# One-core decoder layer: mixer pieces in a new order, the first piece multiplied unsplit, weight halves split ahead of each evacuation, every head transposed during the next

## The reference

```python
def rmsnorm(t, g):
    t32 = t.astype(jnp.float32)
    t32 = t32 * lax.rsqrt(jnp.mean(t32 * t32, axis=-1, keepdims=True) + EPS)
    return (t32 * g.astype(jnp.float32)).astype(t.dtype)
...
    for _ in range(DEPTH):
        xn = rmsnorm(h, g_mix)
        proj = xn @ w_in
        q, k, v, u_pool, q_mem, gate_logits = jnp.split(proj, SPLITS, axis=-1)

        q = rotary(rmsnorm(q.reshape(B, S, DA_HEADS, 2, DA_HEAD_DIM), q_norm), cos, sin)
        k = rotary(rmsnorm(k.reshape(B, S, DA_HEADS, 2, DA_HEAD_DIM), k_norm), cos, sin)
        v = v.reshape(B, S, DA_HEADS, DA_V_DIM)
        o = diff_attention(q, k, v, lam)
        o = rmsnorm(o, g_subln) * (1.0 - LAMBDA_INIT)
        y_attn = o.reshape(B, S, V_DIM) @ w_b_attn

        y_pool = multiscale_pool(u_pool, pool_w, pool_scale) @ w_b_pool

        y_mem = memory_cross_attention(q_mem, mem, g_mem, w_mem_kv, mq_norm, mk_norm) @ w_b_mem

        g = jax.nn.sigmoid((gate_logits + b_gates).astype(jnp.float32)).reshape(B, S, N_BRANCHES, D)
        merged = (g[:, :, 0] * y_attn.astype(jnp.float32)
                  + g[:, :, 1] * y_pool.astype(jnp.float32)
                  + g[:, :, 2] * y_mem.astype(jnp.float32)).astype(h.dtype)
        h = h + merged @ w_out

        h = h + moe(rmsnorm(h, g_ffn), w_router, b_router, w_gate, b_gate,
                    w_up, b_up, w_down, b_down)
```

## Time and profile before

| | us |
|---|---|
| median of 3 runs | 1284.41 |
| lowest, highest | 1283.96, 1288.04 |
| the profiled execution, its own time | 1283.99 |
| its span, first to last instruction | 1280.7 |
| PE busy | 1174.9 (92%) |
| DVE busy | 464.4 (36%) |
| ACT busy | 251.4 (20%) |
| DMA, mean over the span | 358 GB/s |

### The profile page before, as it was taken

One profiled execution on the slowest core, in us unless ns is written; L12 is line 12 of the kernel. 1 busy time (PEld: TensorE's weight loads), 2 busy tenths in 40 slices (PEclk: granted clock), 3 DMA queues, 4 the chain that ended last, 5 costly groups with the idle time before them and its releaser, 6 DMA issues.

```text
span 1280.7 us, 13937 instructions
## 1 busy us (share of the span) xinstructions
PE 1174.9 (92%) x5444; PEld 589.1 (46%) x5444; DVE 464.4 (36%) x814; ACT 251.4 (20%) x378; POOL 20.8 (2%) x29
## 2 busy tenths in 40 slices
PE   6998999997899999999999999999999999999997
PEld 5786787775643343434334343434434333333332
DVE  7669778874531212122122222212221212212131
ACT  5443555542111010001001010100100010001100
POOL 0200000010000000000000000000000000000000
PEclk9998999998899999999999999999999999999999
DMA  8454454386679999999999999999999999999996
GB/s 317 173 172 149 137 199 165 132 295 230 278 293 420 387 404 428 427 431 427 427 431 427 427 431 427 427 431 427 427 431 427 427 431 427 427 431 427 427 431 285
DMA packets 54824, 458.50 MB, mean 358 GB/s; under 512 B 4304, under 2 KB 5200, under 8 KB 30224
## 3 DMA queue, kind: packets, MB, share of 16 engines
q1 hardware_dynamic: 53408, 454.15, 85.9%
q0 software_dynamic: 1104, 3.93, 0.9%
q10 hardware_dynamic: 288, 0.10, 0.0%
HBM read 457.11 MB, written 1.05 MB: 358 GB/s over the span
## 4 chain that ended last, share of the span: by engine, by line
PE 68%; DMA 16%; DVE 10%; ACT 3%; issue 2%; SPq 0%; DVEq 0%; ACTq 0%
PE bank L1496 29%; DMA experts_ring<-in_w_down 14%; PE bank L1548 14%; PE bank L1254 12%; PE bank L1516 5%; PE bank L1484 3%; DVE ring_split L776 3%; PE bank L1502 2%; ACT region L746 1%; PE bank L1223 1%; PE bank L1503 1%; DMA ring<-in_w_in 1%; DVE region L1174 1%; ACT prob L651 1%; ACT region L749 1%
## 5 line engine op out<-in xcount | busy, mean ns | idle before, releaser
L1496 PE MATMUL bank<-experts_ring,region 128*64 128x512 f32 x2048 | 454.0, 595 | 11.5 <-DVE region L1183 6.6
L1496 PEld LDWEIGHTS bank<-experts_ring,region 128*64 128x64 f32 x2048 | 145.0, 137 | 291.7 <-issue 286.8
L1548 PE MATMUL bank<-experts_ring,region 128*64 128x512 f32 x1024 | 228.8, 596 | 31.8 <-ACT region L746 25.0
L1254 PE MATMUL bank<-ring_split,region_split 128*128 128x512 f32 x768 | 233.7, 406 | 18.0 <-DVE ring_split L776 11.0
L1254 PEld LDWEIGHTS bank<-ring_split,region_split 128*128 128x128 f32 x768 | 146.8, 195 | 52.7 <-DVE ring_split L776 12.7
L1548 PEld LDWEIGHTS bank<-experts_ring,region 128*64 128x64 f32 x1024 | 73.1, 137 | 167.0 <-issue 125.8
L1254 PE MATMUL bank<-ring_split 128*128 128x512 f32 x288 | 114.7, 398 | 0.0
L1208 DVE COPY region<-bank 64x512 f32<-64x512 f32 x32 | 22.2, 694 | 237.0 <-PE bank L1548 237.0
L1191 DVE TENSOR_SCALAR region<-bank 128x512 f32<-128x512 f32 x32 | 22.1, 692 | 209.7 <-PE bank L1503 209.7
L776 DVE TENSOR_TENSOR ring_split<-ring,ring_split 128x2048 fp32r<-128x2048 f32 x42 | 95.7, 2288 | 0.3
L1198 DVE TENSOR_SCALAR region<-bank 128x512 f32<-128x512 f32 x32 | 22.1, 692 | 179.7 <-PE bank L1503 179.7
(11 more groups left out here) (167 smaller groups left out, 615.9 us busy)
## 6 DMA issues: line engine op xcount, KB each, us to landing
experts_ring<-in_w_gate SPq DMA_DIRECT2D x64, 2048.0 KB, 25.9
experts_ring<-in_w_up SPq DMA_DIRECT2D x64, 2048.0 KB, 25.1
experts_ring<-in_w_down SPq DMA_DIRECT2D x64, 2048.0 KB, 27.9
ring<-in_w_in SPq DMA_DIRECT2D x28, 1024.0 KB, 5.2
ring<-in_w_mem_kv SPq DMA_DIRECT2D x4, 1024.0 KB, 12.4
ring<-in_w_b_attn SPq DMA_DIRECT2D x4, 1024.0 KB, 5.1
ring<-in_w_out SPq DMA_DIRECT2D x4, 1024.0 KB, 5.0
region<-in_b_gates POOLq DMA_DIRECT2D x6, 512.0 KB, 5.2
```

Of the source, the lines that this page charges most:

```text
L1254: ins = nc.tensor.matmul(UB[u % 3][:, :], a[:, k, toks], b[:, cols], start=(k == 0 and m == 0), stop=(k == k_n - 1 and m == 2))
L1496: ins = nc.tensor.matmul(dst[h * SLOTS:(h + 1) * SLOTS, :], XE[:, kk, e * SLOTS:(e + 1) * SLOTS], w[:, k, h * HALF:(h + 1) * HALF], start= ...
L1548: ins = nc.tensor.matmul(bank[2][h * SLOTS:(h + 1) * SLOTS, :], AHT[:, k, half * SLOTS:(half + 1) * SLOTS], w[:, k, h * HALF:(h + 1) * HAL ...
```

## The change

The pieces are taken in another order. `SPLIT_AT` puts both parts of a half's split (`hi_after`, `lo_after`) ahead of a unit's evacuation, where they stood behind it. The first piece isn't split: its 16 matmuls take x and the weights in plain float32, and x itself is split by ACT (upper) and DVE (lower) later. Sums of squares come from ACT (`square_evac`), the inverse roots of all groups from POOL (`inverse_root`: an addition and a power), in place of ACT's root and DVE's reciprocal. For q the factor isn't multiplied in but given to the exponential as its scale. A head's outcome is squared by ACT, rooted by POOL, scaled out by ACT (`o_squares`, `o_out`), and transposed by PE in the following head's pass (`turn_o`). In the mixer's end, ACT's splits of the last halves go behind its copies of the merged sum, and unit 44 is cut in two with the last transposition between.

```diff
-PIECES = ["pool", "mk", "mv", "qm", "q0", "q1", "k0", "k1", "v0", "v1", "gp0", "gp1", "wbp",
+PIECES = ["pool", "mk", "q0", "mv", "q1", "qm", "k0", "v0", "k1", "v1", "gp0", "gp1", "wbp",
...
-UPPER_AT, LOWER_AT = {}, {}
+SPLIT_AT = {}
 for _n in range(len(PIECES)):
     _second = LAST_UNIT[_n]
     _first = _second - (2 if PIECES[_n] in ("wbp", "wbm") else 1)
-    for _at, _u, _H in ((UPPER_AT, _first, 2 * _n + 4), (UPPER_AT, _second, 2 * _n + 5),
-                        (LOWER_AT, _first, 2 * _n + 3), (LOWER_AT, _second, 2 * _n + 4)):
+    for _u, _H in ((_first, 2 * _n + 3), (_second, 2 * _n + 4)):
         if _H < 2 * len(PIECES):
-            _at[_u] = _H
+            SPLIT_AT[_u] = _H
+NORMED = [u for u, (n, name, t, c) in enumerate(UNITS) if name in ("mk", "qm", "q0", "q1", "k0", "k1")]
+TURNED = [u for u in NORMED if UNITS[u][1][0] in "qk" and UNITS[u][1] != "qm"]
...
+            def inverse_root(cols, eps, signal):
+
+                n_eps[0] += 1
+                nc.gpsimd.tensor_scalar(cols, cols, eps, None, ALU.add).then_inc(eps_added, 1)
+                pool.wait_ge(eps_added, n_eps[0])
+                nc.gpsimd.tensor_tensor(cols, cols, minus_half.to_broadcast([P, cols.shape[1]]), ALU.pow).then_inc(signal, 1)
...
+            def o_root(h):
+                pool.wait_ge(o_squared, 2 * h + 2)
+                inverse_root(stat[:, 128 + 2 * h:130 + 2 * h], EPS, o_scale_ready)
+
+            for h in range(3):
+                o_root(h)
...
+            def square_evac(u, dst):
+
+                _, name, t, _ = UNITS[u]
+                n = 1 if name == "mk" else 0
+                r = NORMED.index(u)
+                act.wait_ge(unit_done, u + 1)
+                act.wait_ge(inv_ready, n + 1)
+                if r >= 2:
+                    act.wait_ge(sq_read, r - 1)
+                else:
+                    act.wait_ge(squares, 4)
+                nc.scalar.activation(SQ[:, r % 2, :], UB[u % 3][:, :], ACT.Square,
+                                     scale=stat[:, 2 * n + t:2 * n + t + 1]).then_inc(sq_done, 1)
+                evac(u, dst)
...
+            def hi_after(u):
+                if u in SPLIT_AT:
+                    hi(SPLIT_AT[u])
...
+            def o_squares(h):
+
+                act.wait_ge(pv_done, h + 1)
+                for t in range(NT):
+                    g = 128 + 2 * h + t
+                    if h or t:
+                        act.wait_ge(o_squared, 2 * h + t)
+                    nc.scalar.activation(O_JUNK, bank[7][:, t * P:(t + 1) * P], ACT.Square, scale=P ** -0.5,
+                                         accum_out=stat[:, g:g + 1]).then_inc(o_squared, 1)
+
             def o_out(h):
-                act.wait_ge(pv_done, h + 1)
-                nc.scalar.activation(O[:, :, h * P:(h + 1) * P], bank[7][:, 0:256].rearrange("p (t n) -> p t n", t=NT),
-                                     ACT.Copy).then_inc(o_copied, 1)
-
+
+                act.wait_ge(o_scale_ready, h + 1)
+                if h >= 2:
+                    act.wait_ge(oT_done, h - 1)
+                for t in range(NT):
+                    g = 128 + 2 * h + t
+                    nc.scalar.activation(O2[:, h % 2, t, :], bank[7][:, t * P:(t + 1) * P], ACT.Copy,
+                                         scale=stat[:, g:g + 1]).then_inc(o_copied, 1)
+
+            def oT(h):
+                act.wait_ge(oT_done, h + 1)
+                nc.scalar.activation(OT[0][:, h, :], bank[6][:, 0:SEQ], ACT.Copy, scale=sub_gain).then_inc(oT_copied, 1)
+
...
+                if h:
+                    o_squares(h - 1)
+                hi_after(a)
+                if h:
+                    o_out(h - 1)
                 if h + 1 < HEADS:
                     exps(h + 1)
...
+                aT(h)
+                gate_exp_of(a)
                 if h + 2 < HEADS:
...
+                hi_after(b)
+                gate_exp_of(b)
+                if h:
+                    oT(h - 1)
+            o_squares(HEADS - 1)
+            hi_after(37)
+            o_out(HEADS - 1)
+            gate_exp(37)
...
+            hi_after(42)
+
+            def mgT(j):
                 act.wait_ge(mgT_done, j + 1)
...
+            mgT(0)
+            mgT(1)
+            hi_after(43)
+            mgT(2)
+            mgT(3)
+            hi_after(44)
...
+            def group_sums(u):
+
+                r = NORMED.index(u)
+                width = MHD if UNITS[u][1] in ("mk", "qm") else HD
+                dve.wait_ge(sq_done, r + 1)
+                nc.vector.tensor_reduce(group_cols(u), SQ[:, r % 2, :].rearrange("p (m n) -> p m n", n=width), AX_X,
+                                        ALU.add).then_inc(sq_read, 1)
+
+            def normed_by(u, rows3, width, groups, signal):
+
+                dve.wait_ge(group_inv, NORMED.index(u) + 1)
+                nc.vector.scalar_tensor_tensor(out=rows3, in0=rows3, scalar=width ** 0.5, op0=ALU.mult, op1=ALU.mult,
+                                               in1=group_cols(u).unsqueeze(2).to_broadcast([P, groups, width])).then_inc(signal, 1)
+
+            def key_norm(u):
+                normed_by(u, KM[:, UNITS[u][2], :].rearrange("p (h n) -> p h n", n=MHD), MHD, MHEADS, mem_normed)
+
+            def rotate(u):
...
+                link(nc.vector.tensor_tensor(a, raw, rot[:, w, 0, t, :].unsqueeze(1).to_broadcast([P, 8, HD]), ALU.mult))
+                if w == 0:
+                    nc.vector.tensor_tensor(raw, a, b, ALU.add).then_inc(normed, 1)
+                else:
+                    link(nc.vector.tensor_tensor(raw, a, b, ALU.add))
+                    normed_by(u, raw, HD, 8, normed)
...
             def unit(u):
+                lo_after(u)
                 (add_bias if UNITS[u][1][0] == "g" else merge)(u)
-                split_next(u)
...
-            mean_square(3, slice(4, 5), D)
             route(0)
             weigh(0)
-            norm_h(0)
             add_h(47)
             copy_hT(3, 1, 1)
-            dve.wait_ge(squares, 6)
-            mean_square(4, slice(5, 6), D)
+            norm_h(0)
...
+                    if H < EARLY:
+                        if k % 4 == 0:
+                            pe.wait_ge(raw_in[H], 16)
+                            pe.wait_ge(xT_copied, 2 * t + k // 4 + 1)
+                        ins = nc.tensor.matmul(UB[u % 3][:, :], XNT[2][:, k, toks], raw(H)[:, cols], start=(k == 0), stop=(k == k_n - 1))
+                        if k == 3 and t == NT - 1:
+                            ins.then_inc(first_half_used, 1)
+                        continue
...
-            unit(9)
+
+            def turn_kq(j):
+                rows_, t = ((KM, 0), (KM, 1), (QM, 0), (QM, 1))[j]
+                if j < 2:
+                    pe.wait_ge(mem_normed, j + 1)
+                else:
+                    pe.wait_ge(bank_read[(8 + j) % 3], (8 + j) // 3 + 1)
+                turn4(bank[(3, 6, 4, 5)[j]], [rows_[:, t, h * P:(h + 1) * P] for h in range(MHEADS)], kq_done)
+
+            unit(6)
+            turn_kq(0)
+            turn_kq(1)
+            unit(7)
             for j in range(2):
...
 
+            mem_scores(0)
+            mem_scores(1)
             unit(14)
-            unit(15)
-            mem_scores(0)
-            unit(16)
-            mem_scores(1)
-            unit_k(17, 0, 4)
             mem_turn(0)
...
+            unit_k(15, 0, 4)
             mem_values(0)
+            mem_turn(1)
             mem_scores(2)
-            mem_turn(1)
...
+            def turn_o(h):
+                pe.wait_ge(o_copied, 2 * h + 2)
+                pe.wait_ge(at_copied, min(h + 2, HEADS))
+                if h:
+                    pe.wait_ge(oT_split, h)
+                for t in range(NT):
+                    ins = nc.tensor.transpose(bank[6][:, t * P:(t + 1) * P], O2[:, h % 2, t, :], ident)
+                ins.then_inc(oT_done, 1)
+
...
                     turn_qk(h + 2)
-                if h == HEADS - 1:
-                    values(h)
-                unit(23 + 2 * h)
-                if h < HEADS - 1:
-                    values(h)
+                unit(22 + 2 * h)
+                if h:
+                    turn_o(h - 1)
+                values(h)
+            unit(37)
+            turn_o(HEADS - 1)
             unit(38)
...
-            for j in range(4):
-                t, h = divmod(j, 2)
-                pe.wait_ge(o_normed, t + 1)
-                turn4(bank[3 + j], [O[:, t, (4 * h + b) * P:(4 * h + b + 1) * P] for b in range(4)], oT_done)
-            pe.wait_ge(oT_split, 2)
+            pe.wait_ge(oT_split, HEADS)
...
             turn_merged(2)
+            pe.wait_ge(mgT_split, 1)
+            unit_k(44, 0, 4)
             turn_merged(3)
             pe.wait_ge(mgT_split, 3)
-            unit(44)
+            unit_k(44, 4, KD)
```

520 lines of the change are left out of this document (247 added, 273 removed).

## The result

The changed kernel takes 1244.40 us (median of 4 runs, 1243.35 to 1245.17) where the kernel before took 1286.22 (1283.96 to 1288.43): ratio 0.9674, 95% interval 0.9652 to 0.9697. In a later comparison the same two stood at 1244.18 and 1285.06 (ratio 0.9682, 0.967 to 0.9695), 41 us. The direction was right; the gain is 14 us larger than the 27.6 that I forecast.

What follows compares the result with a forecast made beforehand. Transfers bound the experts; PE, with 32.4 us of stops, sets the mixer's pace, and the end follows the mixer. Terms 0 − 11.0 − 3.6 − 0.4 − 0.5 − 2.4 − 10.2 − 1.0 + 1.5 = −27.6: 1283.99 to 1256.4 us, range 1246 to 1269.

Steps and rivals of the forecast that it cites:

- Clock: PE's slow clock behind stops: −3.6 us behind two waits for lower parts, 1.4 more at the merge's end.
- Rival 5: More than forecast: all stops but the first and the router's go, with memory and head waits; 1248 us, chance 0.08.
- Attention heads: Head loop: DVE's pace stays in heads with short units, so only −0.5 us of 4.3 us of waits.
- My sign of being wrong: One of three signs against the forecast: in the head loop, heads with short units last over 10 us.
- Memory heads and new waits: Memory heads: most of the waits stay, −0.4 us. New waits at `turn_qk(0)`, `mem_scores(0)` and POOL's roots: +1.5 us.
- Lower parts: Mixer: PE's four waits for L776 go, as DVE's lower part stands ahead of the next evacuation: −11.0 us.
- Rival 4: DVE becomes the bound of the new q, k, memory stretch, giving back 7.5 us: 1264 us, chance 0.12.
- Start: PE's first unit: begins earlier, −3.6 us, unsplit matmuls cost +2.9, possibly low clock up to +1.6; taken as 0.
- Merge's end: Mixer's end: ACT's last splits between and behind its copies remove PE's 8.8 us of stops, 1.4 of clock: −10.2 us.
- Outcomes of the heads and router: Only one head left at the end of the heads: −2.4 us. Router's entry, `norm_h(0)` behind `add_h(47)`: −1.0 us.
- Rival 1: POOL's roots come late beside DVE's L776, 2.4 us in each of 4 short-unit heads: 1266 us, chance 0.13.
- Rival 2: The head's new chain sets the pace, lengthening each of 4 short passes: 1294 us, slower, chance 0.04.

Runs made afterwards that it cites:

- the five variants of the kernel before: Kernel before, one edit each: ACT's order at merge's end 1279.76 us, lower parts ahead 1286.76, DVE lighter 1274.96, needless matmuls in a stop 1284.66, x by tiles 1284.82.
- the one with a stop of 4.6: Changed kernel with ACT's splits of the last two halves of w_out put back ahead of all four copies of the merged sum: 1249.76 us.
- the filled one: Kernel before with 14 needless matmuls in front of the last transposition of the merged sum, where PE stood: 1284.66 us.
- the faster version: Changed kernel with DVE's lower parts behind the merge for units 42 and 43, and `norm_h(0)` in two halves around `add_h(47)`: 1242.25 us.

## Why the prediction was wrong, step by step

*Clock: the largest miss, 6.1 of 11.6 us.* The mechanism was right, that slow clock goes with the stops, and its size was wrong: I took 5.0, from three windows, and 11.1 went. The kernel before had more such windows, which I could have read:

```profile
12.00:16.00 4.00, 3.81 (x10) 3.01 (x11) 3.93 (x6) 3.41 (x5) 0.00 (x0) 0.57 1.04 391
120.00:124.00 4.00, 4.00 (x15) 3.18 (x15) 3.18 (x4) 1.78 (x4) 0.00 (x0) 0.80 0.00 0
280.00:284.00 4.00, 4.00 (x14) 3.17 (x14) 1.83 (x3) 3.07 (x3) 0.00 (x0) 0.75 1.11 328
...
344.00:356.00 12.00, 7.12 (x32) 6.51 (x33) 7.58 (x40) 1.98 (x3) 0.00 (x0) 0.50 1.02 435
```

The whole of it was 12.5 us before and 1.4 after. It isn't tied to one stop: the five variants of the kernel before lost 10.3 to 14.3 with the first unit counted in, at partly other places. Some of these places differ though the instructions up to them are the same: 32 to 38 us in this trace, 56 to 62 in three variants whose edits come later. The changed kernel's variants without a stop over 2.1 us between the first unit and the router lost 1.4 to 3.4, all in the router, and the one with a stop of 4.6 lost 3.0 behind it besides. So one stop less gave back 2.2 us at most (the filled one), and all of them nearly everything. That a cured stop's loss moves to another stop is a reading of these sums, not shown in itself. With 11.1 in place of 5.0 my forecast would have been 1250.3, inside the range, and the rest of the miss lies in the heads, the memory and the waits that didn't come. Rival 5, at 1248, had these right and lacked the same clock.

*Attention heads: 3.1 us.* I took DVE's pace in short heads, 9.3 us for four heads, as staying. The step overlooked that the loop takes the units one earlier, which mixes short with full ones. Putting that back cost 10 us; how much of the 3.6 it made is open. My sign of being wrong, short heads of over 10 us, has lost its sense: a pass with one short and one full unit lasts 10.4 to 11.1.

*Memory heads and new waits: 3.0 us.* `turn_qk(0)` and `mem_scores(0)` wait for nothing; the only wait there is 0.7. Which edit took the memory heads' 1.9 no run here parts.

*Lower parts: the size right (11.1 for 11.0), the reason wrong.* The place in DVE's queue alone only moved the waits. For the two later ones (1.7 and 4.4) it was DVE's 6.45 us for a tile against PE's 5.47; the two earlier ones (2.3 and 2.7) stayed when the tiles got lighter, and which edit took those no run here parts. Rival 4, that DVE would stay the bound, fell for the same reason, as both the load and the order had changed.

*Start: right.* The first unit starts at 8.5, and the unsplit piece costs 3.1 more on PE, with 2.9 forecast. It ran at full clock (14.0 us for 16, 0.875 each), so the allowance for a low one wasn't needed. I did not see that the waits for x were split by tile.

*Merge's end: 1.7 us less than forecast,* which are the two waits for L1054, one of them 1.1 us and so over the 1 us that I had named: DVE's lower part of the half before the last stands ahead of the merge. I had named that as a risk, and the faster version takes it away.

*Outcomes of the heads and router: as forecast* within 0.5. For the router that has some luck in it: I took half of L776's time, 1.1 us, for `norm_h(0)`, and it takes DVE 2.1 in both traces (338.70 before, 304.56 after); the wait for it went from 1.6 to 0.8. What took the 2.4 at the outcomes wasn't tried alone.

*Rival 1, POOL's roots.* The trace does have the blocked instruction. POOL in order of time, after, with DVE's lower part from 38.44 to 40.72 beside it, and the same form 3 us later, beside a shorter DVE instruction (L906, 41.97 to 42.66):

```profile
38.61 2.21 POOL L483 TENSOR_SCALAR stat<-stat 128x4 f32<-128x4 f32 x1 [11.45 <-DVE stat L900]
...
42.02 0.74 POOL L483 TENSOR_SCALAR stat<-stat 128x4 f32<-128x4 f32 x1
```

Each ends 0.1 behind DVE's instruction; alone such an addition takes 0.23 (at 82.21). That agrees with the rule that I quoted from the Trainium skill, "SBUF — State Buffer", section "🔬 SBUF: two separate sides". But of the 24 roots only this one and the router's last (2.30 us for a power of one column, 0.58 for the one before) show it at this size. In the eight roots of q and k it is small. One of them, POOL and then DVE:

```profile
47.67 0.35 POOL L483 TENSOR_SCALAR stat<-stat 128x8 f32<-128x8 f32 x1 [3.80 <-DVE stat L900]
48.10 1.67 POOL L485 TENSOR_TENSOR stat<-stat,small 128x8 f32<-128x8 f32 x1
```

```profile
48.17 0.69 DVE L928 TENSOR_TENSOR tmp<-region,rot 128x512 f32<-128x512 f32 x1
```

The addition stands under a DVE product of 0.41 and takes 0.35 to 0.40, again ending 0.1 behind it. The power starts first, and beside it nothing is longer: DVE's product takes the 0.69 that it takes elsewhere, and 1.67 continues the 0.71 of 2 columns and the 1.03 of 4 in a straight line. There an exclusive lock isn't seen, and the measurement decides. Rival 1 was a question of how often and how long, and I had assumed 1.97 us for each of a root's two instructions, every time.

*Rival 2* was wrong for this kernel, but with the old pairing the heads did cost some 10 us more, most of it in waits of its chain.
